# Two-layer hybrid model on one core: 34 input chunks a layer split in a high and a low part, decay preparation moved, router on centred tiles

## The reference, cut to what matters

```
h = rms_norm(x); u = h @ w_in
u_conv, c_q, c_kv, k_rope, hq, hf, hi, hg, u_gate = split(u)
y_a = silu(layer_norm(causal depthwise conv, 31 taps, of a * sigmoid(g))) @ w_conv_out
y_b = latent attention of c_q, c_kv, k_rope (8 heads), @ w_attn_out
y_c = gated linear recurrence of hq, hf, hi, hg (decay, 4 heads), @ w_hgrn_out
x = x + (gates0*y_a + gates1*y_b + gates2*y_c) @ w_out
x = x + square(relu(rms_norm(x) @ w_ff1)) @ w_ff2
```

```
h = layer_norm(alpha*h + y)
g_logits = h @ wr_g + br_g          # one group a token
e_logits = h @ wr_e + br_e          # two experts in it
y = sum of the chosen experts, down(silu(gate) * up)
```

## Time and profile before

| | us |
|---|---|
| median of 3 runs | 2446.72 |
| the profiled execution's own time | 2448.65 |
| its span | 2446.7 |
| PE busy | 2274.3 (93%) |
| DVE busy | 1513.4 (62%) |
| ACT busy | 1070.5 (44%) |
| POOL busy | 234.6 (10%) |

### The profile page before, as it was taken

One profiled execution on the slowest core, in us unless ns is written; L12 is line 12 of the kernel. 1 busy time (PEld: TensorE's weight loads), 2 busy tenths in 40 slices (PEclk: granted clock), 3 DMA queues, 4 the chain that ended last, 5 costly groups with the idle time before them and its releaser, 6 DMA issues.

```text
span 2446.7 us, 36644 instructions
## 1 busy us (share of the span) xinstructions
PE 2274.3 (93%) x13888; PEld 1896.9 (78%) x13888; DVE 1513.4 (62%) x2353; ACT 1070.5 (44%) x1514; POOL 234.6 (10%) x225
## 2 busy tenths in 40 slices
PE   7999999999999999999999679999999797999997
PEld 6677567899767856789977379888888477988886
DVE  3846265755384626575534566888775166788876
ACT  1142433344114244234432236666654264667665
POOL 1814000101181400010100000000000000000000
PEclk9999799999999989999999689999999898999999
DMA  4332123455333212355533035888854412688884
GB/s 163 125 121 77 44 69 130 164 177 170 119 129 121 79 44 69 130 181 189 184 129 105 28 118 197 300 296 308 293 206 170 140 44 102 213 309 300 307 296 144
DMA packets 109807, 396.86 MB, mean 162 GB/s; under 512 B 12088, under 2 KB 14144, under 8 KB 109376
## 3 DMA queue, kind: packets, MB, share of 16 engines
q1 hardware_dynamic: 108576, 393.45, 47.1%
q10 hardware_dynamic: 1056, 1.06, 0.1%
HBM read 393.40 MB, written 1.06 MB: 161 GB/s over the span
## 4 chain that ended last, share of the span: by engine, by line
PE 76%; DVE 15%; ACT 5%; issue 2%; DMA 1%; SPq 0%; DVEq 0%; ACTq 0%
PE psum L534 75%; DVE W_LO L1565 3%; DVE region L1570 2%; PE psum L542 1%; DVE region L1573 1%; DVE RS L1602 1%; DMA ring<-in_weights 1%; ACT region L1183 1%; DVE X_LO L1570 1%; ACT W_HI L1178 1%; DVE region L1577 1%; DVE SQ L1570 1%; ACT L1187 1%; ACT SQ L1183 1%; ACT XT L1183 1%
## 5 line engine op out<-in xcount | busy, mean ns | idle before, releaser
L1565 DVE TENSOR_TENSOR W_LO<-ring,W_HI 128x1024 fp32r<-128x1024 f32 x434 | 531.9, 1226 | 223.7 <-ACT W_HI L1178 211.8
L1178 ACT ACTIVATE W_HI<-ring 128x1024 fp32r<-128x1024 f32 x434 | 461.6, 1064 | 343.9 <-PE psum L534 239.2
L534 PE MATMUL psum<-HN,ring 128*128 128x272 f32 (+1 forms) x1600 | 383.3, 401 | 16.0 <-DVE HN L1577 16.0
L534 PEld LDWEIGHTS psum<-HN,ring 128*128 128x128 f32 x1600 | 310.1, 196 | 84.5 <-issue 24.8
L534 PE MATMUL psum<-X_HI,W_HI 128*128 128x256 f32 x800 | 229.2, 286 | 18.6 <-DVE W_LO L1565 16.8
L534 PE MATMUL psum<-X_LO,W_HI 128*128 128x256 f32 x800 | 224.0, 280 | 0.0
L534 PE MATMUL psum<-X_HI,W_LO 128*128 128x256 f32 x800 | 224.0, 280 | 0.0
L1187 ACT ACTIVATE region<-psum 128x272 f32<-128x272 f32 (+9 forms) x227 | 89.9, 396 | 286.0 <-PE psum L534 266.3
L1565 DVE TENSOR_TENSOR W_LO<-SQ,W_HI 128x1024 fp32r<-128x1024 f32 x128 | 156.9, 1226 | 37.2 <-ACT W_HI L1178 32.1
L534 PEld LDWEIGHTS psum<-X_HI,W_HI 128*128 128x128 f32 x800 | 152.4, 191 | 23.8 <-issue 19.8
L534 PE MATMUL psum<-W_HI,XG_HI 128*128 128x512 f32 x384 | 153.6, 400 | 17.3 <-DVE W_LO L1565 15.3
(11 more groups left out here) (297 smaller groups left out, 4276.2 us busy)
## 6 DMA issues: line engine op xcount, KB each, us to landing
ring<-in_weights SPq DMA_DIRECT2D x615, 512.0 KB, 4.2
SQ<-in_weights SPq DMA_DIRECT2D x128, 512.0 KB, 4.8
XT<-in_x SPq DMA_DIRECT2D x1, 1088.0 KB, 4.9
CST<-in_consts SPq DMA_DIRECT2D x1, 1082.5 KB, 7.1
SQ<-bias_by_distance ACTq DMA_DIRECT2D x1, 1024.0 KB, 5.4
out<-XT SPq DMA_DIRECT2D x8, 128.0 KB, 1.9
PAR<-in_params SPq DMA_DIRECT2D x1, 572.0 KB, 8.1
bias_by_distance<-MIX ACTq DMA_DIRECT2D x1, 12.0 KB
```

The costliest lines, as they stand in the source:

```text
L534: ins = nc.tensor.matmul(dst, w, x, start=start, stop=stop, skip_group_check=True)
L1178: lane(nc.scalar.activation(W_HI[:, s % SPLIT, :], ring_slot(n), ACT.Copy), split_hi)
L1565: lane(nc.vector.tensor_tensor(W_LO[:, s % SPLIT, :], ring_slot(n), W_HI[:, s % SPLIT, :].bitcast(F32), ALU.subtract), split_lo)
```

## The change

Five things. (1) In the first block 34 chunks a layer go from whole to split: a1 to g3 (6), cq, ckv, rope (4), the 24 gates. `norm(2l)` makes HN_HI (ACT) and HN_LO (DVE); the whole normed tiles are HN[0], now in SQ. (2) `conv_in` places its splits by hand and starts 16 taps between them; GpSimd's product is in TAP. (3) `hgrn_prep` comes ahead of `hi_in`, and `conv_norm` ahead of `mla_in`; `conv_silu` and the two latents are steps of their own among the gates. (4) The router's weights are multiplied by the layer norm's gain at the start (GpSimd), gain and bias are folded into an offset RC (TensorE); TensorE multiplies the centred tiles (`router_rows`), DVE applies the root to the logits, and two tiles at a time are scaled between the small steps. X_HI is now a copy on ACT, X_LO stays on DVE and moves into `moe_lead`. (5) `limit` looks at whether the slot's former chunk had begun, and steps in LATER run one chunk less ahead.

The parts below follow the order of the file: the Follower's limit, the tiles, then TensorE (`start`, `gate`, `router_rows`, `router`), ScalarE (`norm`, `conv_in`), VectorE (`norm`, `conv_in`, `hgrn_prep`, `layer_norm`, `router` and `order`, `moe_lead`), GpSimd (`start`, `hgrn_args`), and the schedule. `conv_gated` is the product of a and the gate, `some_taps(l, lo, hi)` the taps lo to hi - 1 of the 93, `ln_scale` the scaling of some tiles, `x_low` their X_LO; the `follow.to` of `hgrn_prep` stands on ScalarE ahead of the Exp, on VectorE ahead of the strip arguments.

```diff
+LATER = ("conv_norm", "conv_var", "latent", "gate", "conv_silu", "hgrn_clamp", "hgrn_args", "branch_out", "hgrn_block", "hgrn_turn", "hgrn_values",
+         "mla_up", "hgrn_norm", "hgrn_gates", "hgrn_spread", "head_norm", "head_spread", "att_scores", "att_norm", "att_turn", "att_values")
...
-        count = min(begun - 1 + SPLIT, len(self.chunks))
-        while count and self.chunks[count - 1] > n - 2 + RING and self.before[self.chunks[count - 1]] not in self.known:
+        count = min(begun - 1 + SPLIT - lag, len(self.chunks))
+        while count and self.chunks[count - 1] > n - 2 + RING and self.known.get(self.before[self.chunks[count - 1]], begun) >= begun:
...
+        HN = [SQ[:, : KT * T].rearrange("p (k t) -> p k t", k=KT), MIX[:, :, :]]
+        TAP = HAT[:, 0, 0, :T]
+        CQ_ROOT = HAT[:, 0, 1, :T]
+        LOGITS = SQ[:20, 2048:2304]
...
-            hn = lambda k: HN[:, k, :]
+            hn = lambda k: (HN_HI[:, k, :], HN_LO[:, k, :])
+            whole = lambda r: lambda k: HN[r % 2][:, k, :]
...
+                for l in range(DEPTH):
+                    dst, done = take("router_offset", l)
+                    mm(dst[:, :20], ones(1, 128), par(f"rbias{l}", 1), True, False)
+                    for k in range(KT):
+                        shift = par(f"lnb0_{l}")[:, k : k + 1].to_broadcast([128, 128])
+                        mm(dst[:, :20], shift, par(f"router{l}")[:, 20 * k : 20 * k + 20], False, k == 7, done if k == 7 else None)
...
-                project(("gate", l, b, m), lambda k: HN[:, k, at:], T - at)
+                project(("gate", l, b, m), lambda k: (HN_HI[:, k, at:], HN_LO[:, k, at:]), T - at)
...
+            def router_rows(l):
+                pe.wait_ge(sem("router_scaled"), l + 1)
+                dst, done = take("router_rows", l, bank=2)
+                for k in range(KT):
+                    if k == KT - 1:
+                        mm(dst[:20, :256], par(f"router{l}")[:, 20 * k : 20 * k + 20], ht(k), False, True, done)
+                    else:
+                        w = par(f"router{l}")[:, 20 * k : 20 * k + 20]
+                        ins = nc.tensor.matmul(dst[:20, :256], w, ht(k), start=k == 0, stop=False, skip_group_check=True)
+                        ins.then_inc(sem("router_read"), 1)
...
+            def router(l):
+                pe.wait_ge(sem("logits"), l + 1)
+                for i in range(2):
+                    dst, done = take("router", l, i, bank=i)
+                    turn(dst[:, :20], LOGITS[:, 128 * i : 128 * i + 128], 20, done)
...
+                if r % 2 == 0:
+                    for k in range(KT):
+                        act.wait_ge(sem("normed"), KT * r + k + 1)
+                        fn(HN_HI[:, k, :], HN[0][:, k, :], ACT.Copy, sem("norm_hi"))
...
+                    wait_bank("conv_a", l, j)
+                    follow.to(first + min(2 * j + 2, 6))
...
+                    for k in range(KT):
+                        dve.wait_ge(sem("norm_hi"), KT * (r // 2) + k + 1)
+                        tt(HN_LO[:, k, :], HN[0][:, k, :], HN_HI[:, k, :].bitcast(F32), ALU.subtract, sem("norm_split"))
...
+                follow.to(first + 2)
+                conv_gated(l, 0)
+                follow.to(first + 3)
+                some_taps(l, 0, 3)
+                follow.to(first + 4)
+                some_taps(l, 3, 4)
+                conv_gated(l, 1)
+                some_taps(l, 4, 5)
+                follow.to(first + 5)
+                some_taps(l, 5, 8)
+                follow.to(first + 6)
+                conv_gated(l, 2)
+                some_taps(l, 8, 16)
+                conv_gated(l, 3)
...
+                follow.to(splits.first["mla_in", l] + 1)
...
+                ln_scale(r, range(2))
+                src = wait_bank("router_rows", l)
+                ins = nc.vector.tensor_tensor(LOGITS[:, :], src[:20, :256], RS[:20, :256], ALU.mult)
+                lane(ins, sem("logits"))
+                free(nc.vector.memset(SM[:, 31:32], 0.0), "router_rows", l)
+                ln_scale(r, range(2, 4))
...
-                split_x(2 * l, range(5))
...
-                    free(nc.vector.tensor_copy(RT[:, 20 * i : 20 * i + 20], src[:, :20]), "router", l, i)
+                    free(nc.vector.tensor_tensor(RT[:, 20 * i : 20 * i + 20], src[:, :20], RC[:, 20 * l : 20 * l + 20], ALU.add), "router", l, i)
...
-                split_x(2 * l, range(5, KT))
+                ln_scale(2 * l, range(4, 6))
...
                 lane(nc.vector.tensor_copy(ORD[:, :], MS[:, 28:32]), sem("order"))
+                ln_scale(2 * l, range(6, KT))
...
+                x_low(l, range(2))
+                follow.to(first("gate", 0) + 1)
+                x_low(l, range(2, 4))
+                follow.to(first("gate", 0) + 2)
+                x_low(l, range(4, KT))
...
+            def start():
+                for l in range(DEPTH):
+                    banks.await_(pool, ("router_offset", l))
+                    for k in range(KT):
+                        w = par(f"router{l}")[:, 20 * k : 20 * k + 20]
+                        lane(nc.gpsimd.tensor_scalar(w, w, par(f"lng0_{l}")[:, k : k + 1], None, ALU.mult), sem("router_scaled") if k == 7 else None)
...
+                if i == 2:
+                    banks.await_(pool, ("ckv_var", l))
...
-        s += [("conv_in", l), ("conv_taps", l), ("hgrn_in", l), ("mla_in", l), ("conv_norm", l)]
-        s += [("gate", l, 0, 0), ("conv_var", l), ("mla_norm", l), ("hgrn_prep", l)]
-        s += [("gate", l, 0, m) for m in range(1, KT)] + [("hgrn_clamp", l, 0), ("hgrn_clamp", l, 1), ("hgrn_args", l, 0)]
+        s += [("conv_in", l), ("conv_taps", l), ("hgrn_in", l), ("hgrn_prep", l), ("hi_in", l), ("conv_norm", l), ("mla_in", l)]
+        s += [("conv_var", l), ("mla_norm", l), ("gate", l, 0, 0), ("latent", l, 0), ("gate", l, 0, 1), ("gate", l, 0, 2), ("latent", l, 1)]
+        s += [("gate", l, 0, 3), ("conv_silu", l)] + [("gate", l, 0, m) for m in range(4, KT)] + [("hgrn_clamp", l, 0), ("hgrn_clamp", l, 1), ("hgrn_args", l, 0)]
```

168 lines of the change are left out of this document (108 added, 60 removed).

## The result

The kernel after takes 2463.64 us (median of 10 runs, 2454.77 to 2465.86), the kernel before 2449.69 (10 runs of it, 2445.35 to 2456.7). The ratio is 1.005, 95% interval 1.0037 to 1.0063: slower by half a per cent, 27 us above the forecast of 2437 and outside its range. The profiled execution took 2463.5, with a span of 2461.7.

What follows compares the result with a forecast made beforehand. TensorE, busy 93% of the span, bounds except where DVE and ACT chains end last. Layer 0 0.0, layer 1 -2.2, routers -10.6, clock +3.4: together -9.4 us, forecast 2437 from a median of 2446.72, range 2402 to 2456.

Steps and rivals of the forecast that it cites:

- What a split is worth: Per chunk on TensorE: 0.70 us saved at 272 columns, 0.65 at 256; 46.4 us in all if nothing waits.
- Projections, layer 0: conv_in of layer 0: 4.2 us saved, mostly lost waiting for the second W_LO; -0.4, bounds -4.2 and +3.
- Layer 1's start: conv_in of layer 1: chunks save 4.2 us, two W_HI ahead of norm's squares cost 2 x 1.06; net -2.1.
- Taps to gates 0: Taps, decay preparation, latents, gates 0: savings less 8.7 us of new waits; -4.3 layer 0, -4.8 layer 1.
- Decay blocks: Gates 1: W_LO between mask and clamp lengthens the serial chain; +3.5 us a layer, bounds -2 and +14.
- +0.8 for five blocks: Decay blocks: W_LO adds 1.23 us, part returned by a clamp clear of GpSimd; +0.8 taken for five blocks.
- -2.0 credited to a TensorE: Decay blocks: 2.0 us a layer gained where TensorE still leads.
- rival that the blocks grow: Decay blocks: each W_LO meets GpSimd's product, TensorE falls to half clock; +14 us a layer, end 2469; chance 0.14.
- SBUF rule: Decay blocks: two-SBUF-input DVE and GpSimd instructions exclude each other; W_LO beside GpSimd would bring the upper bound, +14 us.
- Gates 2: Branch 2 gates: waits at the root and at gate 5 outweigh 5.6 us saved; +1.2 a layer, bounds -5.6 and +6.
- Router: Both routers: scaling to order 7.5 us instead of 14.2; gain 5.3 a layer, 10.6 in all, bounds 4 and 15.
- Clock: Half clock after the new wait at gate 6, 1.7 us in each layer: +3.4, bounds 0 and +14.

Runs made afterwards that it cites:

- bounds_later: As paying, but lower bound step, bucket bias and its DMA moved behind conv_in, only the first latent chunk split in hgrn_prep: 0.9901, 2425.3 us.
- paying: Kernel after with gates of branches 1 and 2 whole, offset products ahead of head_norm(0), second conv_in split ahead of start, cq0 and cq1 splits in hgrn_prep: 0.9950, 2437.4 us.
- mla_only: Kernel after with conv_in and all 24 gates a layer whole, only cq, ckv and rope split, offset products ahead of head_norm(0): 0.9940, 2434.0 us.
- gates1_behind: Kernel after with W_LO of the decay block gates made behind the clamp on DVE instead of ahead of it: 1.0033, 2455.9 us.
- best2: Start, offset and cq edits of paying, all 34 splits kept; in decay blocks W_LO behind the clamp, W_HI behind the Exp, one gate further ahead: 1.0020, 2455.8 us.
- gates1_short: Kernel after with the 16 decay block gates whole (HN_HI alone), only six of each gate's eight products: 0.9975, 2445.2 us.
- warm: Kernel after plus eight thrown-away products ahead of the wait of each turn in the decay blocks: 1.0035, 2457.1 us.
- router_only: Kernel before with the router part alone, offset products ahead of the wait for the head squares (hgrn_norm): 0.9949, 2436.9 us.

## Why the prediction was wrong, step by step

By the table, the end came 24.4 later than the sum had it. Three steps make up that miss: the decay blocks 14.3, the start 8.2, the start of layer 1 4.2. The rest makes -2.

- **What a split is worth:** right. Evacuations in gates 0 stand 3.0 apart, and TensorE's work at full clock fell by 37.7 of the 46.4.
- **Projections, layer 0 (-0.4, bounds to +3):** failed, at +7.8. The second W_HI was placed by its count, not by ACT's queue: ahead of it stand a table load, an Exp that waits for DVE, and a DMA waited for until it lands. In six profiles with the same start this costs some 5 us; in this one the landing took 3.3 for their 1.4 to 1.8, and the half clock was long. On the offset the prediction said "DVE is what ends last there, so I cost the offset at nothing". Where the clock held, that was right. It was costed from a row at half clock (7.02 for 32 records; 36 take 4.5 at full clock). That the half-rate stretch "should go" failed: it was there in every profile, 3.4 to 10.3 us long. bounds_later shows what the place of the start step costs with its followers: 12 us against paying.
- **Layer 1's start (-2.1):** failed, at +2.1. The two W_HI ahead of the squares cost 2.2 (the wait there is 2.84 for 0.66), as forecast; another 3.8 between `mix_out` and `conv_in` were not forecast and not taken apart.
- **Taps to gates 0 (-4.3, -4.8):** right (-4.0, -5.0), though the wait at gate 6 didn't come and cq1 cost more. mla_only shows that the splits in gates 0 pay.
- **Decay blocks (+3.5 a layer):** the step that failed most, at +8.7 and +12.6 (81.5 to 81.8 for layer 1 in three other profiles of the same blocks make it +8.2 to +8.5 there). The mechanism was right, W_LO inside the chain, but three terms were wrong. The +0.8 for five blocks was too small: the nine blocks, from mask to mask, took 4.6 and 8.9 more; gates1_behind puts the place of W_LO at some 5 a layer, and best2, with W_HI out of the chain too, brings the blocks back to their old length. The +1.5 for the first block was 3.8: the prediction had W_HI wait for its gate, and not the Exp of `hgrn_args(1)` wait behind W_HI and its weight DMA. And the -2.0 credited to a TensorE that "still leads" was not there: gates1_short shows that its time is worth nothing in the blocks. What the shorter gates free becomes stops, and with them comes half clock (0.88 and 0.84), which warm and best2 show to be the smaller part. The rival that the blocks grow (0.14, +14 a layer, 2469) was nearer in size and named the half clock, but its reason, W_LO meeting GpSimd's product each time, held for one W_LO a layer.
- **The SBUF rule** was cited for the upper bound. A W_LO beside GpSimd's product did take 2.23 for 1.23 (at 238.23, GpSimd from 236.88 to 239.38). By that rule (SBUF — State Buffer, section SBUF: two separate sides, of the Trainium skill) the trace agrees. But most W_LO there ran at 1.23 with GpSimd idle, and the loss came without the rule.
- **Gates 2 (+1.2 a layer):** near in the sum against the kernel before (-2.4, +3.7), but the step was mis-sized. Against whole gates the splits cost some 4 a layer. Something else in the change made this stage shorter; what, was not taken apart.
- **Router (-5.3 a layer):** right, -6.4 and -7.2; in router_only 0.5% for both. Its printed terms add up to 7.8 (or 6.9, if the last scaling is in the 3.1), not 7.5; 7.6 was measured. After each in the kernel after 2.1 and 3.5 were lost again, at half clock or in waits I did not separate.
- **Clock (+3.4, bounds to +14):** failed. TensorE's busy time holds 25.6 more of it. How much of that is span is open, since in the blocks it costs little. The term counted one new stop a layer. There are ten new ones of 2 us or more in the first block (4.2 at the start, 4.4 twice at cq1, four at turns, 3.8 and 3.6 at gate 5, 2.8 at the norm of layer 1), for three that went (3.8 at the start, 2.9 and 4.9 at the first branch product). I added the clock as a term of its own, but it follows from the other terms. The Trainium skill (TensorE: Matmul & The Clock Gate, section HAM oscillation — how this bites in real kernels) describes a case near to this one, pieces of work shorter than the DMA waits between them, so that the clock falls at every wait. The trace agrees in part: the waits here are for DVE, and in layer 0's blocks the clock fell 1.3, 2.1 and 1.3 us after the waits of 1.1, 2.1 and 2.8 had ended, and not at the other turns, whose waits are below 1. I had weighed no rule on the clock.

## What to carry to other kernels

Count a shorter matmul as a gain only where TensorE sets the pace. In a serial chain of other engines it buys a longer stop and perhaps half clock, and its price (here W_HI and W_LO) lands in the chain, or in the queue ahead of it. Before a new instruction is costed as hidden, read its engine's queue in order ahead of it, for DMAs that are waited for and for waits on a third engine. And when a change does forty small things, put each group back alone: here 16 of the 34 splits a layer lost 27 us together, the 6 in `conv_in` lost time only behind the start step, and the 8 in gates 0 won 9 us. And read a stage from several profiles before you explain its length.

## What the runs showed of the hardware

- Where the half clock falls, and for how long, is not fixed by the program. Eight profiles share every instruction of the start (after and seven more). The first half-clock stretch is 3.4 us long in four, 6.8 in two and 10.2 to 10.3 in two, though TensorE stands in no wait from 17.6 on until well behind the first stretch in all of them.
- A stage's length scatters with it. Layer 0's blocks took 82.8, 83.1, 83.1 and 87.5 in kernels that differ only elsewhere, at 0.90, 0.88, 0.88 and 0.86; layer 1's took 85.9, 81.8, 81.5 and 81.5. A stage's length from one profile is good to some 4 us here, and only repeated runs settle the sign.
- How long ACT waits for a DMA to land scatters too: `store_bias`, 12 KB, held the next instruction back until 1.4 to 1.8 us after its issue in six of these profiles and 3.3 in two.
- The clamp on DVE (128x1024) takes 0.69 alone. Before, from 197.0 to 225.8, five of them took 0.97 to 1.69, with 0.4 to 1.1 us of that beside a GpSimd instruction. With W_LO ahead of it, it fell clear and took 0.69, so an instruction put ahead of it can be paid back in part.
